# Products that nobody reads in TensorE's pauses around two routings, two layer norms and an RMS norm

## The chip, the cores and the metric

One Trainium2 chip, one core. The metric is the device time of one execution in microseconds (us). Three executions of the kernel before took 1819.88, 1822.99 and 1823.16 us; their median is 1822.99.

## What is computed

Two transformer blocks run one after the other on 256 tokens of 1024 values, all in float32. The first block mixes tokens with a gated delta rule and a spatial gating unit, and ends in a mixture of 32 experts. The second mixes them with two kinds of attention (16 heads), and ends in a mixture of 16 experts. What matters here is what stands ahead of each mixture:

```
x  = x + gate * merge_branches(...) @ w_o           # first block
hx = modulate(rms_norm(x, norm_ffn_g), shift, scale)
x  = x + gate * hier_moe(hx, ...)                   # 32 experts, 2 of them for each token
x  = rms_norm(x, final_norm_g)

h = token_mixer(x, ...)                             # second block
x = layer_norm_2(ALPHA * x + h, ln1_g, ln1_b)
h = grouped_moe(x, ...)                             # 16 experts, 2 of them for each token
x = layer_norm_2(ALPHA * x + h, ln2_g, ln2_b)
```

The two experts of a token are found from router logits (a product of the tokens with 36 or 16 columns), softmax and comparisons.

## The kernel before

Tokens lie along the free axis and the 1024 values in eight tiles (`KT = 8`) of 128 partitions. `X` holds the residual, `H` and `HS` the normed tokens and the squares. TensorE (`pe`), VectorE (`dve`), ScalarE (`act`), GpSimd (`pool`) and the DMA queue of SyncE (`sp`) each have a program of their own, written out by hand; semaphores (`s[...]`, `wait_ge`, `then_inc`) order them. TensorE executes its matmuls in the order of its program: whatever is put ahead of a wait is done before what stands behind it.

Every matmul goes through the helper `mm`, so that all of them have line L601 in the profile. A float32 product is two passes there: two LDWEIGHTS and two MATMULs.

Weights stream through a ring of nine slots of 1 MB (`ring`). `sp` loads the next slot when TensorE has released it (`slots_used`); with all nine full the queue stands still. The rows of experts that are chosen by rank are loaded only after VectorE has written the order (`order_ready`, L1818), in `count_tokens`.

The stretches that the change touches, in order of time:

- **First routing and gather**, `route(0, ...)` and the head of `mixture(0)`. After the last `norm_sum(0, 7)` ScalarE and VectorE make `H`, and a DMA brings `router_w`. TensorE then makes the logits (16 products with 36 columns, and two for the bias), 16 transposes of 128x128 (L958), waits for `kept` (L1887: the experts that each token keeps), makes five small products into bank 6 (`placed`), and waits while `place_tokens` and `make_gather` (L1828 to L1949) work out on VectorE which token goes where. `gather_x(0)` (16 products with 128 columns) collects the tokens of the first unit, VectorE and ScalarE copy them, and `up(0, 0)` and `up(0, 1)` begin the experts' work.
- **The first block's last norm**: eight `norm_sum(1, k)` (256 columns each, from L2043 by way of ScalarE's squares), then ScalarE and VectorE (L2048) norm `X`, and the second block's projections begin.
- **Attention's end**: four products with `sq_att` (512 columns), ScalarE's `heads_rnorm`, then the output projections, eight products each.
- **Second block's layer norm and routing**: `mean_sum(0, k)`, `variance_sum(0)`, then `route(1, ...)` and `mixture(1)`, built as the first. `X` comes from VectorE at L2137.
- **The last layer norm**: `mean_sum(1, k)`, `variance_sum(1)`, and the result is stored.

Bank 7 of PSUM is written by `gather_x` and `down`, and read only after these.

Of the kernel before, what the change touches and what calls it, by code (L numbers as in the profile page):

```python
# [211 lines left out]
def build(nc, t):  # L212

    ctx = ExitStack()
    with ctx:
        def sb(name, *shape):
            return ctx.enter_context(nc.sbuf_tensor(name, [P, *shape], F32))
# [10 lines left out]
        mats = sb("mats", len(MATS), P)  # L228
        ones = sb("ones", P)
# [8 lines left out]
        bank = [ctx.enter_context(nc.psum_tensor(f"bank{i}", [P, 512], F32)) for i in range(8)]  # L238
# [6 lines left out]
        def M(name):  # L245
            return mats[:, MATS.index(name), :]
# [352 lines left out]
        def _(pe):  # L599
            def mm(out, lhsT, rhs_, start=True, stop=True, **kw):  # L600
                return nc.tensor.matmul(out, lhsT, rhs_, start=start, stop=stop, **kw)  # L601
# [3 lines left out]
            def release(ins):  # L605


                nonlocal group_ended
                if group_ended:
                    ins.then_inc(slots_used, 1)  # L610
                group_ended = False
# [26 lines left out]
            def project_rows(acc, w, src, first):  # L638
# [6 lines left out]
                            release(ins)  # L645
                return ins

            def column_sum(out, src, n=KT):

                for k in range(n):  # L650
                    ins = mm(out, ones[:, :], src[:, k, :], k == 0, k == n - 1)
                    if k == 0:
                        release(ins)
                return ins

            pe.wait_ge(s["constants_set"], 4)

            pe.wait_ge(s["xc_squared"], 1)
            column_sum(bank[1][:, :], hc).then_inc(s["xc_summed"], 1)

            pe.wait_ge(s["cond_ready"], 1)
# [208 lines left out]
            n = 0  # L870
# [46 lines left out]
            def norm_sum(i, k):  # L917

                pe.wait_ge(s["norm_ready"], KT * i + k + 1)
                ins = mm(bank[4][:, 0:SEQ], ones[:, :], HS[:, k, :], k == 0, k == KT - 1)  # L920
                release(ins)
                if k == KT - 1:
                    ins.then_inc(s["norm_summed"], 1)
# [15 lines left out]
            def route(m, width, experts):  # L939


                pe.wait_ge(s["router_landed"], 16 * (m + 1))
                src = H if m == 0 else X
                logits = [bank[5][:, qt * width:(qt + 1) * width] for qt in range(QT)]
                for k in range(KT):
                    pe.wait_ge(s[f"route_in{m}"], k + 1)
                    for qt in range(QT):
                        mm(logits[qt], src[:, k, qt * P:(qt + 1) * P], router_w[m][:, k, :], k == 0 and qt == 0, False,
                           skip_group_check=True)
                at = D + (0, GROUPS1 + E1)[m]  # L950
                for qt in range(QT):
                    ins = mm(logits[qt], ones[0:1, :], one_row[0:1, 0, at:at + width], False, qt == QT - 1, skip_group_check=True)
                ins.then_inc(s["logits_made"], 1)

                for qt in range(QT):
                    for k in range(KT):
                        i = qt * 2 + k // 4
                        ins = nc.tensor.transpose(bank[i][:, (k % 4) * P:(k % 4 + 1) * P], src[:, k, qt * P:(qt + 1) * P],  # L958
                                                  M("ident"))
                        if k % 4 == 3:  # L960
                            ins.then_inc(s["rows_turned"], 1)

                pe.wait_ge(s["kept"], m + 1)
                pe.wait_ge(s["attn_landed"], 16)
                mm(bank[6][:, 0:experts], earlier, keep[:, 0, 0:experts])
                mm(bank[6][:, experts:2 * experts], earlier, keep[:, 1, 0:experts], True, False)
                mm(bank[6][:, experts:2 * experts], ones[:, :], keep[:, 0, 0:experts], False, True)
                mm(bank[6][:, 2 * experts:3 * experts], ones[:, :], keep[:, 0, 0:experts], True, False)
                mm(bank[6][:, 2 * experts:3 * experts], ones[:, :], keep[:, 1, 0:experts], False, True
                   ).then_inc(s["placed"], 1)  # L970

            def mixture(m):
# [9 lines left out]
                def gather_x(u):  # L982

                    pe.wait_ge(s["gather_made"], ub + u + 1)
                    for k in range(KT):
                        for qt in range(QT):
                            ins = mm(bank[6 + k // 4][:, (k % 4) * P:(k % 4 + 1) * P], own_rows[:, qt, k * P:(k + 1) * P],
                                     gather[u % 2][:, qt, :], qt == 0, qt == QT - 1)
                        if k % 4 == 3:
                            ins.then_inc(s["x_gathered"], 1)  # L990
# [59 lines left out]
                def combine_y(u):  # L1050
# [7 lines left out]
                                 combine[u % 2], u == 0 and j % 2 == 0, u == UNITS[m] - 1 and j % 2 == 1, skip_group_check=True)  # L1058
                    ins.then_inc(s["combined"], 1)

                pe.wait_ge(s["rows_copied"], 4 * (m + 1))
                gather_x(0)
                up(0, 0)
# [24 lines left out]
            def every_token(m):  # L1088
# [32 lines left out]
                ins.then_inc(s[f"all{m}_pe"], 1)  # L1121

            route(0, GROUPS1 + E1, E1)
            mixture(0)
            for k in range(KT):
                norm_sum(1, k)

            n2 = 0
            for j in range(O20):
# [100 lines left out]

            def variance_sum(i):

                for k in range(KT):
                    pe.wait_ge(s["ln_sq"], KT // 2 * i + k // 2 + 1)
                    ins = mm(bank[5][:, 0:SEQ], ones[:, :], HS[:, k, :], k == 0, k == KT - 1)
                ins.then_inc(s["ln_var"], 1)

            pe.wait_ge(s["heads_rnorm"], 8)
            for j in range(KT):
                if j >= 4:  # L1240
# [4 lines left out]
                if j > 0:  # L1245
                    mean_sum(0, j - 1)
            mean_sum(0, KT - 1)
            variance_sum(0)
            route(1, E2, E2)
            mixture(1)  # L1250
            for k in range(KT):
                mean_sum(1, k)
            variance_sum(1)


# [993 lines left out]
```

## Time and profile before

| | us |
|---|---|
| executions | 1819.88, 1822.99, 1823.16 |
| median | 1822.99 |
| the profiled execution, whole | 1820.98 |
| its span, first to last instruction | 1819.2 |
| TensorE busy | 1633.8 |
| VectorE busy | 553.0 |
| ScalarE busy | 322.6 |
| mean granted TensorE clock | 0.953 |

The page gives each engine's busy time and, in 40 slices of 45.5 us, TensorE's granted clock in tenths of full speed. The views used below are the timeline of TensorE (each line a group of like instructions, with the idle time ahead of it in brackets and what ended it), and the table of stretches, which gives for a stretch the busy time of each engine and the granted clock: 1.00 is 2.4 GHz and 0.50 is 1.2 GHz.

### The profile page before, as it was taken

What the parts mean: (1) busy time and instruction counts of PE and PEld (TensorE: products, weight loads), DVE (VectorE), ACT (ScalarE), POOL (GpSimd) and SP (SyncE); (2) the same over time, 40 slices, a digit from 0 to 9 for tenths busy, and PEclk for the clock granted to TensorE, in tenths of its full rate; (3) what the DMA queues carried; (4) which work ended last, traced back from release to release, by engine and by line L of the source; (5) the groups of instructions that cost most, each with busy time, mean ns of one, the idle gap of its engine ahead of it and who ended that gap; (6) DMA issues with size and microseconds to landing.
All of it is one profiled execution on the core that took longest, in us unless ns stands there. A gap on an engine that the chain in (4) does not pass through costs nothing.

```text
span 1819.2 us, 21572 instructions
## 1 busy us (share of the span) xinstructions
PE 1633.8 (90%) x8392; PEld 1057.2 (58%) x8392; DVE 553.0 (30%) x1120; ACT 322.6 (18%) x648; POOL 174.0 (10%) x180
## 2 busy tenths in 40 slices
PE   5799999999999989969998789988799998999985
PEld 1466666776588868855554369757534543443433
DVE  2266666666520011153122110382511111011002
ACT  2223333333231100011001021241100000000001
POOL 1144333334300000000000000000000000000000
PEclk8799999999999978969999899899699999999999
DMA  9311110111834413418999974103299989999993
GB/s 392 145 52 46 35 46 27 43 46 35 337 114 162 142 67 123 147 54 349 421 421 420 421 278 161 48 1 120 88 409 422 395 349 422 421 359 387 421 422 158
DMA packets 59644, 404.91 MB, mean 223 GB/s; under 512 B 6782, under 2 KB 7938, under 8 KB 13232
## 3 DMA queue, kind: packets, MB, share of 16 engines
q1 hardware_dynamic: 53328, 381.92, 52.7%
q0 software_dynamic: 6240, 21.92, 4.0%
q8 instruction: 55, 0.90, 0.2%
q14 instruction: 21, 0.17, 0.0%
HBM read 402.71 MB, written 1.10 MB: 222 GB/s over the span
## 4 chain that ended last, share of the span: by engine, by line
PE 70%; DMA 16%; DVE 9%; issue 2%; ACT 1%; SPq 0%; DVEq 0%; POOL 0%; POOLq 0%; ACTq 0%
PE bank L601 69%; DMA ring<-in_moe 14%; DVE arena L1619 2%; DMA ring<-in_dense 2%; ACT arena L1261 1%; DVE arena L1650 1%; DVE arena L1666 1%; PE bank L1017 1%; DVE arena L1655 0%; DVE arena L1647 0%; DVE arena L1645 0%; DVE arena L1659 0%; DMA arena<-in_router_w 0%; DMA arena<-decay_rows 0%; DVE arena L1669 0%
## 5 line engine op out<-in xcount | busy, mean ns | idle before, releaser
L601 PE MATMUL bank<-ring,arena 128*64 128x512 f32 (+2 forms) x2304 | 521.5, 606 | 58.6 <-DMA ring<-in_moe 56.9
L601 PE MATMUL bank<-arena 128*128 128x128 f32 (+3 forms) x2864 | 426.5, 300 | 35.2 <-DVE arena L1949 14.6
L601 PEld LDWEIGHTS bank<-arena 128*128 128x128 f32 (+2 forms) x2864 | 379.0, 194 | 134.0 <-ACT arena L1261 47.8
L601 PEld LDWEIGHTS bank<-ring,arena 128*64 128x64 f32 (+2 forms) x2304 | 174.6, 138 | 369.9 <-issue 364.9
L1261 ACT ACTIVATE arena<-bank 128x256 f32<-128x256 f32 (+1 forms) x369 | 164.1, 451 | 1186.0 <-PE bank L601 892.1
L601 PE MATMUL bank<-hc,head_w 128*128 128x512 f32 (+1 forms) x384 | 166.3, 541 | 3.0 <-DMA head_w<-in_head_w 3.0
L1971 DVE TENSOR_TENSOR arena<-arena,bank 128x256 f32<-128x256 f32 x48 | 20.2, 422 | 360.7 <-ACT arena L1261 360.7
L601 PE MATMUL bank<-arena,ring 128*128 128x256 f32 x512 | 116.6, 388 | 4.3 <-ACT arena L1261 2.6
L601 PEld LDWEIGHTS bank<-arena,ring 128*128 128x128 f32 x512 | 99.7, 195 | 19.7 <-ACT arena L1261 3.4
L601 PE MATMUL bank<-hc,ring 128*128 128x256 f32 x512 | 110.7, 380 | 0.0
L601 PEld LDWEIGHTS bank<-hc,ring 128*128 128x128 f32 x512 | 97.5, 190 | 12.9
L601 PEld LDWEIGHTS bank<-hc,head_w 128*128 128x128 f32 x384 | 66.2, 200 | 32.6 <-issue 30.3
L1261 ACT ACTIVATE arena<-arena 128x512 f32<-128x512 f32 (+3 forms) x152 | 73.9, 511 | 44.2 <-DVE arena L1871 13.1
L1967 DVE COPY arena<-bank 128x512 f32<-128x512 f32 x21 | 14.5, 692 | 210.9 <-PE bank L601 210.9
L550 POOL TENSOR_TENSOR arena<-arena,mats 128x512 f32<-128x512 f32 x48 | 68.3, 1430 | 103.3 <-PE bank L601 55.4
L1666 DVE TENSOR_TENSOR arena<-bank,mats 128x512 f32<-128x512 f32 x80 | 53.9, 689 | 49.5 <-PE bank L601 47.8
L1619 DVE SCALAR_TENSOR_TENSOR arena<-arena,vec 128x512 f32<-128x512 f32 (+1 forms) x72 | 62.6, 869 | 6.5 <-DVE arena L1617 1.2
L601 PE MATMUL bank<-xc,ring 128*128 128x256 f32 x256 | 55.7, 380 | 1.6 <-DVE xc L2048 1.6
L601 PEld LDWEIGHTS bank<-xc,ring 128*128 128x128 f32 x256 | 48.6, 190 | 8.4 <-issue 2.0
L601 PE MATMUL bank<-hc,ones 128*128 128x256 f32 (+1 forms) x80 | 27.6, 492 | 20.2 <-ACT hc L1261 20.2
L601 PE MATMUL bank<-arena,ones 128*128 128x512 f32 (+3 forms) x76 | 30.4, 521 | 9.9 <-ACT arena L1261 9.9
L1261 ACT ACTIVATE hc<-xc 128x256 f32<-128x256 f32 (+2 forms) x25 | 15.0, 613 | 128.7 <-DVE xc L1766 116.8
(241 smaller groups left out, 1056.7 us busy)
## 6 DMA issues: line engine op xcount, KB each, us to landing
ring<-in_moe SPq DMA_DIRECT2D x288, 1024.0 KB, 13.2
ring<-in_dense SPq DMA_DIRECT2D x72, 1024.0 KB, 7.0
head_w<-in_head_w POOLq DMA_DIRECT2D x27, 512.0 KB, 4.0
arena<-decay_rows POOLq DMA_DIRECT2D x16, 256.0 KB, 4.6
xc<-in_xc SPq DMA_DIRECT2D x1, 2048.0 KB, 8.6
arena<-bias_rows POOLq DMA_DIRECT2D x2, 1024.0 KB, 8.5
mats<-in_square SPq DMA_DIRECT2D x1, 1088.0 KB, 11.6
out_y<-xc SPq DMA_DIRECT2D x2, 512.0 KB, 2.9
```

Source lines behind the costliest of these rows:

```text
L550: nc.gpsimd.tensor_tensor(levels[k % 2], coupling, times(M(f"off{k}"), TT), ALU.mult).then_inc(s["level_masked"], 1)
L601: return nc.tensor.matmul(out, lhsT, rhs_, start=start, stop=stop, **kw)
L1017: ins = nc.tensor.transpose(bank[4 + step_no % 2][:, f * P:(f + 1) * P], hid[step_no % 2][:, f * P:(f + 1) * P], M("ident"))
L1261: return nc.scalar.activation(out, in_, func, **kw)
L1619: link(stt(c3, src, wgt, c3, ALU.mult, ALU.add))
L1650: stt(flat(conv[0]), flat(conv[0]), float(P) ** -0.5, flat(norms[0]), ALU.mult, ALU.mult).then_inc(s["normed"], 1)
L1666: tt_(group_of(picked, g), grown(g), times(M(f"pick{k + 1}"), 4), ALU.mult).then_inc(s["picked"], 1)
L1967: cp(x_cols[u % 2][:, 4:8, :].rearrange("p a b -> p (a b)"), bank[7][:, :]).then_inc(s["x_copied"], 1)
L1971: tt_(hid[step_no % 2], act_h[step_no % 2], bank[4 + step_no % 2][:, FS:2 * FS], ALU.mult).then_inc(s["hid_ready"], 1)
```

## The change

A helper `keep_warm(n)` does n products of `ones` (128x128) with 512 columns of the constant `mats`, into bank 7, with no wait and no semaphore; nobody reads the bank in between. It is called in eight places of TensorE's program, two of them in `route` and one in `mixture`, which each run twice, and one in `variance_sum`, which runs twice too: 22 products in all. No other engine's program changes.

```diff
+            def keep_warm(n):
+
+                for _ in range(n):
+                    mm(bank[7][:, :], ones[:, :], mats[:, 0:4, :].rearrange("p a b -> p (a b)"))
@@ route
+                keep_warm(2)
                 pe.wait_ge(s["router_landed"], 16 * (m + 1))
@@
+                keep_warm(1)
                 pe.wait_ge(s["kept"], m + 1)
@@ mixture
+                keep_warm(5)
                 pe.wait_ge(s["rows_copied"], 4 * (m + 1))
                 gather_x(0)
@@
             route(0, GROUPS1 + E1, E1)
             mixture(0)
+            keep_warm(1)
             for k in range(KT):
                 norm_sum(1, k)
+            keep_warm(1)
@@
             def variance_sum(i):
 
+                keep_warm(1)
                 for k in range(KT):
@@
+            keep_warm(2)
             pe.wait_ge(s["heads_rnorm"], 8)
             for j in range(KT):
```

## Rows read from the trace of the kernel before

**Rows 1.** The page: span, and TensorE's granted clock in 40 slices.
```profile
span 1819.2 us, 21572 instructions
...
PEclk8799999999999978969999899899699999999999
```

**Rows 2.** Stretches (start:end length, engines' busy us, clock, DMA share, GB/s).
```profile
790.00:820.00 30.00, 17.60 (x83) 14.37 (x84) 18.66 (x77) 4.29 (x8) 0.00 (x0) 0.65 0.00 1
...
827.00:1049.00 222.00, 199.46 (x1230) 106.99 (x1229) 48.44 (x111) 21.24 (x44) 0.00 (x0) 0.97 1.01 417
...
1275.00:1308.00 33.00, 24.22 (x112) 21.15 (x114) 18.94 (x79) 4.50 (x7) 0.00 (x0) 0.59 0.00 0
```

**Rows 3.** TensorE's timeline, first routing and gather (start, length, instruction, idle before).
```profile
778.35 0.70 PE L601 MATMUL bank<-hc,ones 128*128 128x256 f32 x2 [0.59 <-ACT hc L1261]
783.28 7.04 PE L601 MATMUL bank<-arena,hc 128*128 128x36 f32 x32 [4.24 <-DMA arena<-in_router_w]
...
791.25 3.40 PE L958 MATMUL bank<-mats,hc 128*128 128x128 f32 x16
797.55 1.00 PE L601 MATMUL bank<-arena,head_w 128*128 128x32 f32 x4 [2.90 <-DVE arena L1887]
...
808.54 6.75 PE L601 MATMUL bank<-arena 128*128 128x128 f32 x32 [8.71 <-DVE arena L1949]
```

**Rows 4.** Stretches of the first routing, with the clock.
```profile
780.00:781.00 1.00, 0.00 (x0) 0.00 (x0) 0.96 (x1) 0.01 (x1) 0.00 (x0) 0.79 0.92 385
...
783.28:791.25 7.97, 7.96 (x36) 7.83 (x37) 2.01 (x6) 0.00 (x0) 0.00 (x0) 0.50 0.14 59
...
794.00:795.00 1.00, 0.65 (x5) 0.41 (x3) 0.86 (x5) 0.00 (x0) 0.00 (x0) 0.88 0.00 0
...
799.85:808.54 8.69, 0.00 (x0) 0.03 (x1) 7.62 (x28) 0.14 (x1) 0.00 (x0) 0.50 0.00 0
```

**Rows 5.** Timeline at full clock: 128 columns; a weight load ahead of 512 columns.
```profile
823.10 3.84 PE L601 MATMUL bank<-arena 128*128 128x128 f32 x32
...
827.64 0.19 PEld L601 LDWEIGHTS bank<-arena,ones 128*128 128x128 f32 x1 [0.24 <-issue]
```

**Rows 6.** TensorE's timeline, the first block's last norm.
```profile
1062.65 5.41 PE L601 MATMUL bank<-hc,ones 128*128 128x256 f32 x16 [2.15 <-ACT hc L1261]
1069.68 27.87 PE L601 MATMUL bank<-xc,ring 128*128 128x256 f32 x128 [1.62 <-DVE xc L2048]
```

**Rows 7.** TensorE's timeline, attention's end and the output projection.
```profile
1227.46 3.70 PE L601 MATMUL bank<-arena,mats 128*128 128x512 f32 x8 [1.24 <-DVE arena L2117]
1233.74 8.86 PE L601 MATMUL bank<-arena,ring 128*128 128x256 f32 x32 [2.58 <-ACT arena L1261]
...
1242.87 3.62 PE L601 MATMUL bank<-arena,ring 128*128 128x256 f32 x16
```

**Rows 8.** TensorE's timeline, second layer norm, routing and gather.
```profile
1268.98 3.72 PE L601 MATMUL bank<-hc,ones 128*128 128x256 f32 x16 [1.86 <-ACT hc L1261]
1275.58 6.98 PE L601 MATMUL bank<-arena,xc 128*128 128x16 f32 x32 [2.88 <-DVE xc L2137]
...
1288.70 1.03 PE L601 MATMUL bank<-arena,head_w 128*128 128x16 f32 x4 [1.56 <-DVE arena L1930]
...
1296.86 6.65 PE L601 MATMUL bank<-arena 128*128 128x128 f32 x32 [5.85 <-DVE arena L1949]
```

**Rows 9.** Timeline of VectorE: the last tiles that the second router reads.
```profile
1277.58 1.38 DVE L2137 TENSOR_SCALAR xc<-xc,vec 128x256 f32<-128x256 f32 x4
```

**Rows 10.** Stretches within a run of products with 32 columns, early in the kernel.
```profile
52.00:56.00 4.00, 4.00 (x38) 4.00 (x37) 0.00 (x0) 0.00 (x0) 0.00 (x0) 1.00 1.00 418
57.00:59.00 2.00, 2.00 (x11) 2.00 (x11) 0.00 (x0) 0.00 (x0) 0.00 (x0) 0.50 0.42 172
```

**Rows 11.** TensorE's timeline, the last layer norm.
```profile
1800.31 3.72 PE L601 MATMUL bank<-xc,ones 128*128 128x256 f32 x16 [1.75 <-DVE xc L2144]
1805.90 3.72 PE L601 MATMUL bank<-hc,ones 128*128 128x256 f32 x16 [1.86 <-ACT hc L1261]
```

## The prediction

> **What bounds the kernel now.** I read the page first: the granted clock is near full in most slices, and lowest (7, 8, 6 of ten) early and where the two routings lie [rows 1]. The table of stretches shows what a routing is: VectorE and TensorE take turns, and the DMA engines move nothing for 30 us in the first and 33 us in the second, since the ring is full [rows 2]. Behind the first routing they run without a pause (share 1.01) for 222 us [rows 2]. So the mixtures are bound largely by transfers, and these restart only when TensorE frees slots and VectorE, behind the gather's copy, gives the experts' order. A microsecond saved before the first slot is freed moves the stream by as much. I count it in full.
>
> The timeline and the clock then show what a microsecond could come from. After 778.35 + 0.70 TensorE has nothing for 4.24 us [rows 3]; the clock falls within that pause (0.79 in its second microsecond), and the router runs at 0.50 [rows 4]. The transposes lift it (0.88 in the microsecond in which they end), the pause for `kept` loses it again, and the gather after 8.71 us of pause starts at half [rows 3, 4]. Its 32 passes take 6.75 us, where 32 of the same shape take 3.84 at full clock [rows 3, 5]. The second routing repeats this [rows 8].
>
> **The price of a product.** Two passes of 512 columns, each spaced by 0.24 + 0.19 = 0.43 us at full clock [rows 5]: 0.86 us; at half clock, by the ratio 6.75 to 3.84 and its limit of two, 1.5 to 1.7 us; I take 1.7. Five are 4.3 us at full and 8.6 at half. They are only free as long as they end before what TensorE waits for. They have no wait, so TensorE can be late but nobody else is held directly; what they write is read by nobody.
>
> **Part by part.** Where a part is given with two bounds, the first is what it can save at most (the clock stays full), the second what it costs if the clock does not move.
>
> - *Two products ahead of the first router.* Pause 4.24 us [rows 3], they fill 1.7 (3.4 at half): hidden. They put off the fall of the clock, which came about 1.6 us into the pause. Most: the 36 passes take 7.97 us at half [rows 4], so 4.0; cost 0. But early in the kernel the clock fell in the midst of 64 passes much like the router's (38 in 4 us, then 11 in 2 us) while TensorE was never idle [rows 10], so it may fall within the router too. I take 1.3.
> - *One ahead of `kept`, twice.* Pauses of 2.90 and 1.56 us [rows 3, 8]. Saves nothing by itself: what follows are five products whose result VectorE takes later. At half it fills 1.7 us, so in the second routing it can be 0.15 late. Bounds 0 and -0.15; I take 0.
> - *Five ahead of the first gather.* Pause 8.71 us; they take 4.3 to 8.6: hidden in every case, by 0.1 us at least. Most: the gather takes 3.7 instead of 6.75 [rows 3, 5], so 3.1. If they start at half clock, as here [rows 4], I expect them to lift it as the transposes did (0.88 in the microsecond in which these end [rows 4]), and they end some 2 us before the gather, which then starts at full. If they start at full they end 4.4 us before it, longer than the pause in which the clock fell ahead of the router. I take 2.0.
> - *One before and one behind the sums of the norm.* Pauses of 2.15 and 1.62 us [rows 6] against 0.86, or 1.7 at half. The 16 passes took 5.41 us, where 16 of that shape take 3.72 after a pause of 1.86 [rows 6, 8]; the clock fell in the first and not in the second. Most 1.7, cost 0.1. I take 1.7: one product leaves 1.3 us of pause.
> - *Two at attention's end.* Pause 2.58 us [rows 7]; two products take 1.7 there (3.4 at half, 0.8 late). The first 32 passes of the output projection took 8.86 us, the next 16 3.62 [rows 7], so 32 take 7.2. Most 1.7, cost 0.8; I take 1.7.
> - *One in the variance sums and two ahead of the second router.* Pauses 1.86 and 2.88 us [rows 8] against 0.86 and 1.7 at full: hidden; at half 3.4 against 2.88, 0.5 late. The sums already ran at full, 3.72. The router's 36 passes took 7.9 us; but the last tiles it reads come at 1277.58 + 1.38 = 1278.96 [rows 9], and eight passes and the bias follow, so at most 3.0. For the same reason as in the first I take 1.3.
> - *Five ahead of the second gather.* The pause is 5.85 us [rows 8]. At full they end 1.5 us early; at half all through they would be 2.7 late; lifted half way, they need between (4.3 + 8.6)/2 = 6.5 and less, 0.6 late. Most: the gather 3.0 shorter; cost 2.7. I take 2.5 less 0.6 = 1.9. Its small products for `placed` end at 1291.01 and VectorE waited some tenths for them; at full they give 0.1.
> - *The last layer norm.* Both sums ran at full, 3.72 us after pauses of 1.75 and 1.86 [rows 11]: 0, and 0 late even at half.
>
> Sum against the profiled execution: 1.3 + 2.0 + 1.7 + 1.7 + 1.3 + 1.9 + 0.1 = 10.0 us. All bounds of savings together are 16.6, all costs 0.1 + 0.15 + 0.8 + 0.5 + 2.7 = 4.3.
>
> **From the profiled execution to the median.** That execution took 1820.98 and its span 1819.2. In it the clock fell at both of the short pauses where it need not: a pause of 2.15 us lost it ahead of the norm's sums, one of 2.58 at attention's end, while 1.75, 1.86 and 1.86 kept it [rows 6, 7, 8, 11]. In other executions the fall can come at other places, so I count these two at half for the median: 10.0 - 1.7 = 8.3. That gives 1822.99 - 8.3 = 1814.7 from the median and 1820.98 - 8.3 = 1812.7 from the profiled one; I take **1814.5**, nearer the median since that is what is measured.
>
> The Trainium skill bears on this last step. Its page "TensorE: Matmul & The Clock Gate", section "Part 1: The HAM clock gate", says that the moments at which the clock may change are not tied to the start of the kernel, so that one kernel shows another number of slow products in each run. By that rule no sum made from one execution holds in full, and the 10.0 would be 8 or less. One trace can't show it; like pauses with unlike ends (2.15 and 1.86 us) agree with it.
>
> **The rivals.**
>
> *The clock is lost again.* The products end early and the rest of the pause still loses it, ahead of both routers and of one gather, or it falls within the router, as it did in [rows 10]. For: the five run at full end 4.4 us ahead of the first gather. Against: they start at half in the trace, and so end late. What is left are the two norm parts at half, 1.7, one gather 2.0 and 1.2 elsewhere: 4.9, so 1818.1.
>
> *The transfers take the gain back.* The first experts' work starts earlier but the stream, at 417 GB/s for 222 us [rows 2], sets the end and starts no earlier. Then only the norms' parts (1.7 at half) and tenths remain: 1821. Against: the engines stand idle for 30 us before, with the ring full, and what restarts them is behind the gather.
>
> *Slower.* The added products run at half and do not lift the clock. Then each stretch keeps its slow matmuls and gets the overruns: 2.7 us ahead of the second gather first of all, then 0.8 and 0.5, in sum 4.3: 1827.3. It decides from the point at which the five need more than 5.85 us and the gather behind them is not faster, that is, when under 2.7 us of it comes back. Against: it rose while TensorE did transposes, from 791.25 to the microsecond at 794 [rows 3, 4].
>
> **How the numbers follow.** Under 0.2% (3.6 us) can't be told from no change. Forecast (6 to 12 us less, 1811 to 1817): 0.62. Clock lost again (1816.5 to 1821): 0.22, of which 0.13 is faster by over 0.2%. Transfers: 0.11, nearly all within 0.2%. Slower: 0.05. Faster 0.76, same 0.19, slower 0.05. The range goes from 1808.5 (the forecast with two more of the 6.6 us up to the bound of the savings, and the favourable executions) to 1820.0, which takes in most of the first rival and leaves out the other two.
>
> **What would show it.** In the profile after: the gathers at 3.7 us in place of 6.75 and 6.65; the norm's 16 passes at 3.7 for 5.41; the output projection's first 32 at 7.2; the clock's slices at the routings up; the router still partly at half; the idle ahead of the second gather gone, with VectorE's L1949 done some tenths before it. The prediction is wrong if the clock does not rise during the five products, if the gathers start at half, or if the stream of transfers restarts as late as before relative to `norm_sum(0, 7)`.

## The result

Five executions of the changed kernel took 1801.98 to 1807.39 us, median 1805.57; five of the kernel before 1816.44 to 1823.16, median 1819.88. The ratio is 0.9922, 95% interval 0.9902 to 0.9943: some 14.3 us less. I had forecast 1814.5 within 1808.5 to 1820.0: a saving of 8.3 us, from a start of 1822.99. The direction was right and the size too small: the measured time lies below the range.

The profiled execution of the changed kernel has a span of 1800.2 us, 19.0 less than the profiled one before. The page (span, granted clock in 40 slices):

```profile
span 1800.2 us, 21660 instructions
...
PEclk8799999999999988989999999999999999999999
```

The slices of the clock in which the two routings lie, 6 and 6 before [rows 1], are 8 and 9. (The 7 and the 8 ahead of the first 6 belong to the spatial gating unit, 637 to 728 us.) The timeline of TensorE (start, length, instruction, idle before) answers to [rows 3]; the products added are the lines that read `mats` and `ones`:

```profile
779.04 1.88 PE L601 MATMUL bank<-mats,ones 128*128 128x512 f32 x4
783.41 5.81 PE L601 MATMUL bank<-arena,hc 128*128 128x36 f32 x32 [2.49 <-DMA arena<-in_router_w]
...
793.62 1.73 PE L601 MATMUL bank<-mats,ones 128*128 128x512 f32 x2
796.45 0.63 PE L601 MATMUL bank<-arena,head_w 128*128 128x32 f32 x4 [1.10 <-DVE arena L1899]
...
797.59 6.24 PE L601 MATMUL bank<-mats,ones 128*128 128x512 f32 x10
807.44 5.44 PE L601 MATMUL bank<-arena 128*128 128x128 f32 x32 [3.62 <-DVE arena L1961]
813.66 7.09 PE L601 MATMUL bank<-ring,arena 128*64 128x512 f32 x32 [0.79 <-DVE arena L1979]
```

The router starts when it did (783.28 before) and takes 1.2 us less, and the gather takes 5.44 us for 6.75: not the 3.7 of full clock. The five products ended 3.6 us ahead of it. The table of stretches (start:end length, busy us of five engines, granted clock, DMA share, GB/s) shows that the clock is full at the pause's end and falls within the gather:

```profile
806.00:807.00 1.00, 0.00 (x0) 0.00 (x0) 0.89 (x4) 0.00 (x0) 0.00 (x0) 1.00 0.00 0
807.50:811.00 3.50, 3.50 (x22) 3.50 (x23) 0.00 (x0) 0.89 (x2) 0.00 (x0) 0.67 0.02 5
```

The norm and attention's end, for [rows 6, 7], and the second routing, for [rows 8]:

```profile
1057.82 3.72 PE L601 MATMUL bank<-hc,ones 128*128 128x256 f32 x16 [1.29 <-ACT hc L1273]
...
1221.71 7.17 PE L601 MATMUL bank<-arena,ring 128*128 128x256 f32 x32 [0.86 <-ACT arena L1273]
...
1261.88 1.93 PE L601 MATMUL bank<-arena,xc 128*128 128x16 f32 x16 [1.17 <-DVE xc L2149]
1264.34 2.04 PE L601 MATMUL bank<-arena,xc 128*128 128x16 f32 x16 [0.53 <-DVE xc L2149]
...
1280.56 3.81 PE L601 MATMUL bank<-arena 128*128 128x128 f32 x32 [2.20 <-DVE arena L1961]
1285.15 5.37 PE L601 MATMUL bank<-ring,arena 128*64 128x512 f32 x24 [0.78 <-DVE arena L1979]
```

The sums take 3.72 for 5.41, the projection's first 32 passes 7.17 for 8.86, the gather 3.81 for 6.65. The second router now waits for VectorE in its middle (0.53): it ran ahead of it.

Where the 19.0 us between the two spans lie, by how far like instructions are apart: router 1.2, first gather 1.3, norm 1.7, attention's end 1.7, second router 2.5, `placed` and second gather 3.0: 11.4 in the stretches with products. Another 7.9 are elsewhere: 2.4 in the first mixture and 5.5 in attention, 4.5 of these at its entry and 1.0 near its end; 0.3 were lost again here and there. At the entry the first kernel had half clock for 13.7 us and the changed one none:

```profile
1163.00:1176.00 13.00, 12.22 (x28) 7.42 (x28) 6.81 (x14) 4.63 (x9) 0.00 (x0) 0.50 0.00 1
```

```profile
1155.00:1169.00 14.00, 11.24 (x45) 7.20 (x46) 11.89 (x23) 5.88 (x11) 0.00 (x0) 1.00 0.01 1
```

(the first of the kernel before, the second of the changed one). The nearest product that was added ahead of this place ends some 90 us before it.

### The profile page after: what moved, and what is told of

Read it like the earlier page. It is cut to its first block, busy times and chain, and to the rows that moved or that the text cites. A ratio compares the mean times of both kernels' runs of the same rounds, so it can differ in the third digit from the quotient of the medians.

```text
span 1800.2 us, 21660 instructions
## 1 busy us (share of the span) xinstructions
PE 1632.9 (91%) x8436; PEld 1048.4 (58%) x8436; DVE 552.9 (31%) x1120; ACT 323.0 (18%) x648; POOL 173.7 (10%) x180
## 4 chain that ended last, share of the span: by engine, by line
PE 69%; DMA 17%; DVE 9%; issue 3%; ACT 1%; SPq 0%; DVEq 0%; POOL 0%; POOLq 0%; ACTq 0%
PE bank L601 68%; DMA ring<-in_moe 14%; DVE arena L1631 2%; DMA ring<-in_dense 2%; ACT arena L1273 1%; DVE arena L1662 1%; DVE arena L1678 1%; PE bank L1024 1%; DVE arena L1667 0%; DVE arena L1659 0%; DVE arena L1657 0%; DVE arena L1671 0%; DMA arena<-in_router_w 0%; DVE xc L2147 0%; DMA arena<-decay_rows 0%
## 5 line engine op out<-in xcount | busy, mean ns | idle before, releaser
L601 PEld LDWEIGHTS bank<-arena 128*128 128x128 f32 (+2 forms) x2864 | 374.1, 192 | 125.8 <-ACT arena L1273 47.8
L601 PE MATMUL bank<-arena 128*128 128x128 f32 (+3 forms) x2864 | 421.0, 297 | 26.4 <-DVE arena L1681 6.8
```

## The experiments

Each kernel was timed against the kernel before on the same chip. The two theories at the start: **each product acts where it stands**, and its part can be measured alone; or **part of the difference is chance or acts from afar**.

**The kernel before again.** No edit.

> The kernel before, unchanged, profiled a second time. Of the 19.0 us between the two profiled spans some 6 lie where no product was added: 4.0 us at the entry of attention (half clock from 1162.87 for 13.7 us before, full clock after) and 2.3 us at the end of the first mixture (half clock at 1039.99). Theory 1 (chance): those falls come and go between executions of one kernel. Then this profile shows the short falls at other places than the first one; the ones in the two routings stay. Theory 2 (lasting): the kernel before always loses the clock at attention's entry, and the products remove that from afar; then the fall at the entry stands here again. The ratio is 1.000 within 0.2% by both.

Measured: ratio 1.0012 (0.9996 to 1.0028). Half clock stands at attention's entry again:

```profile
1160.20:1173.80 13.60, 12.82 (x30) 7.93 (x30) 7.26 (x14) 4.63 (x9) 0.00 (x0) 0.50 0.00 1
```

This spoke for the second theory. The 29 executions of the kernel before in this comparison have a median of 1817.99, and those of the later ones 1817.4, 1820.0 and 1819.0. The 1822.99 from which I started is the median of three at the upper end.

**The gathers' products alone.** From the changed kernel, all calls but `keep_warm(5)` taken out.

```diff
-                keep_warm(2)          # route
-                keep_warm(1)          # route
                 keep_warm(5)
-            keep_warm(1)              # both of the norm
-                keep_warm(1)          # variance_sum
-            keep_warm(2)              # attention's end
```

> Only the five products ahead of each mixture's first gather (10 of 22). Theory 1 (each product acts where it stands): from the two profiles the gathers gave 1.3 and 2.9 us, so 4 us less than before, ratio 0.9977; the first gather at about 3.8 us for 6.75, the second near 3.8 for 6.65; the routers still at half. Theory 2 (the products act as a whole, or from afar): nearly the full 14 us, ratio 0.992, or nearly none.

Measured: 0.9979 (0.9965 to 0.9993), 3.8 us less, as the first theory has it. Alone, the five bring the first gather to full clock, since they start later and at half, and end 2 us ahead of it:

```profile
806.50 3.81 PE L601 MATMUL bank<-arena 128*128 128x128 f32 x32 [2.04 <-DVE arena L1961]
...
1289.10 3.73 PE L601 MATMUL bank<-arena 128*128 128x128 f32 x32
```

**Without the gathers' products.**

```diff
-                keep_warm(5)
```

> The changed kernel without the five products ahead of each gather (12 of 22 remain). Theory 1 (each acts where it stands): the change's 14.3 us less 4, so about 10 us less than before, ratio 0.9943; both gathers again at 6.7 us. If the whole is worth more than its parts, this and the run with the gathers' products alone give less than 14 us in sum.

Measured: 0.9944 (0.9922 to 0.9967), 10.2 us less. With the 3.8 above it makes the 14 of the whole. I had expected both gathers at 6.7 us. The first takes 5.53 us here, hardly more than the 5.44 with the five: in these profiles the five buy almost nothing at the first gather; at the second they do (6.17 here, 3.81 with them):

```profile
807.64 5.53 PE L601 MATMUL bank<-arena 128*128 128x128 f32 x32 [9.47 <-DVE arena L1961]
...
1284.15 6.17 PE L601 MATMUL bank<-arena 128*128 128x128 f32 x32 [6.75 <-DVE arena L1961]
```

**Narrow products.** All 22 in their places, with 16 columns.

```diff
-                    mm(bank[7][:, :], ones[:, :], mats[:, 0:4, :].rearrange("p a b -> p (a b)"))
+                    mm(bank[7][:, 0:16], ones[:, :], mats[:, 0, 0:16])
```

> All 22 products in their places, each with 16 columns in place of 512: same count of instructions, next to no work for the array. Theory 1 (the work keeps the clock): no gain, ratio 1.000, half clock in both routings. Rival (the gain comes from the instructions ahead of the waits, as that weights are loaded or the queue is filled): 14 us less as with the wide ones.

Measured: 0.9986 (0.9971 to 1.0002), no gain that can be told from none. The router after its narrow products takes its 7.04 us as before, the second gather 6.39. It is the work of the products that holds the clock, not that instructions stand there. Two things did change: the first gather took 5.18 us for 6.75, and attention's entry ran at full, with nothing changed near it. By its span this profile is 6.1 us under that of the kernel before, 4.5 of them at the entry, while the executions together give 2.5 us (none to 5.3). So one profile can overstate a gain.

```profile
783.71 7.04 PE L601 MATMUL bank<-arena,hc 128*128 128x36 f32 x32 [3.87 <-DMA arena<-in_router_w]
...
1291.12 6.39 PE L601 MATMUL bank<-arena 128*128 128x128 f32 x32 [3.72 <-DVE arena L1961]
```

```profile
1160.00:1174.00 14.00, 11.59 (x47) 7.23 (x47) 11.92 (x22) 5.88 (x11) 0.00 (x0) 1.00 0.00 1
```

**The changed kernel again.** No edit.

> The changed kernel, unchanged, measured and profiled again. Its gain on record, 0.9922, rests on five runs of each; the kernel before has now 29 with a median of 1818.0, under the 1819.9 of those five. If the parts add up as they stand (gathers 3.8, all the rest 10.2) the ratio is again 0.9922 to 0.9925. Under the rival that the first five runs happened on favourable positions it is 0.9945 or more. In the profile: both gathers at 3.8 us; a fall at attention's entry may stand or not, no product is near it.

Measured: 0.9925 (0.9911 to 0.9939). The gain on record stands: 13.6 us of 1817.4. The second gather took 3.81 us, but the first 5.44 again, where I had expected 3.8. It is not always so. Two later kernels, the two with eight products ahead of the spatial gating unit, have the same products at the first routing, and its gather took 6.38 us in one profile and 3.81 in the other; with the norm's products alone, and so none anywhere ahead of the gather, it took 5.18 (in this order):

```profile
805.09 6.38 PE L601 MATMUL bank<-arena 128*128 128x128 f32 x32 [5.31 <-DVE arena L1962]
```

```profile
816.22 3.81 PE L601 MATMUL bank<-arena 128*128 128x128 f32 x32 [1.96 <-DVE arena L1963]
```

```profile
806.50 5.18 PE L601 MATMUL bank<-arena 128*128 128x128 f32 x32 [8.80 <-DVE arena L1961]
```

Two things follow. With the five in place, the pause that is left behind them goes with the result: 1.96 and 2.04 us left, 3.81 for the gather; 3.62, 5.44; 5.31, 6.38. And without them the first gather is no fixed point: 6.6 to 6.8 us in five profiles (the kernel before three times, attention's end alone, norm and attention's end), 5.2 in three (norm alone, narrow, variance and `kept` alone). So the 1.3 us between the two profiles at this place can't be credited to the five. The second gather is clear: 3.7 to 3.8 us in all eight profiles with the five or the ten, 5.3 and more in all ten without them or with narrow ones.

**The routers' products alone.**

```diff
                 keep_warm(2)
-                keep_warm(1)          # and the five other calls
```

> Only the two products ahead of each router (4 of 22). From the two profiles the routers gave 1.1 and 2.5 us. Theory 1 (each acts where it stands): 3.5 us less than before, ratio 0.998; router 1 ends about a microsecond earlier after its start at 783.3, router 2 two and a half; the gathers still at 6.7. Rival (the clock falls within the router anyway): under 1 us.

Measured: 0.9985 (0.9976 to 0.9993), 2.7 us less. The rival, under 1 us, is out. The two routers take 6.37 us and 1.93 + 3.14.

**Norm and attention's end alone.**

```diff
-                keep_warm(2)          # route; and those of kept, gather and variance_sum
             keep_warm(1)              # both of the norm
             keep_warm(2)              # attention's end
```

> Only the products around the sums of the first block's last norm (one before, one behind) and the two at attention's end (4 of 22). From the two profiles they gave 1.7 and 1.6 us. Theory 1: 3.3 us less, ratio 0.9982, the sums at 3.7 us for 5.4 and the projection's first passes at full. Rival (in most executions the clock does not fall at these short pauses, as I took for the median): half of that, 1.7 us, 0.9991.

Measured: 0.997 (0.9954 to 0.9986), 5.4 us less, more than the 3.3 to be seen at the two places, though the interval takes 3.3 in. The halving that I used for the median, 1.7 us, lies outside it (2.5 to 8.4). In the profile 1.7 us were lost again behind attention's end: the second block's variance sums took 5.41 us for 3.72. Attention's entry, on the other hand, ran at full there, so more than the two places is in the 5.4.

**The rest alone: one ahead of `kept`, one ahead of the variance sums.**

```diff
-                keep_warm(2)          # route
                 keep_warm(1)          # route
-                keep_warm(5)
-            keep_warm(1)              # both of the norm
                 keep_warm(1)          # variance_sum
-            keep_warm(2)              # attention's end
```

> The rest of the change: only the product ahead of each kept wait and the one ahead of each variance sum (4 of 22). The parts measured so far are 3.8 (gathers), 2.7 (routers) and 5.4 us (norm and attention's end), 11.9 of 13.6. Theory 1 (these four do nothing by themselves, as forecast; the missing 1.7 is uncertainty or comes from the parts acting together): ratio 1.000 to 0.9995. Rival (they carry the missing 1.7 us): 0.999.

Measured: 0.9987 (0.9971 to 1.0002). It decides nothing: 2.4 us less, or none.

**Ten in place of five.**

```diff
-                keep_warm(5)
+                keep_warm(10)
```

> The changed kernel with ten products in place of five ahead of each gather. Ten take 8.6 us at full clock and more where they start at half; the pauses are 8.7 and 5.85 us. Theory (overruns cost one for one): the first gather at most 2 us later, the second 3 to 5 us later, in sum 4 to 6 us more than the changed kernel, ratio 0.9955 to 0.9965. Rival (the stream of transfers has room and takes the delay in, as would be if the transfers bound the mixtures from elsewhere): no change, 0.9925.

Measured: 0.9922 (0.99 to 0.9945), the same as with five, and my theory of 4 to 6 us more fell. Nor was it the rival's room in the transfers. The profile shows a gain and a loss:

```profile
796.11 10.53 PE L601 MATMUL bank<-mats,ones 128*128 128x512 f32 x20
806.47 3.73 PE L601 MATMUL bank<-arena 128*128 128x128 f32 x32
...
1274.91 8.83 PE L601 MATMUL bank<-mats,ones 128*128 128x512 f32 x20
1283.57 3.73 PE L601 MATMUL bank<-arena 128*128 128x128 f32 x32
```

In the first pause they end 0.5 us later than the gather began with five (counted from their own start, the gather begins after 10.4 us for 9.9), and the gather takes 3.73 for 5.44, 1.7 us less. In the second they end 1.9 us later (8.7 for 6.7), where I had expected 3 to 5: they ran at full there. By these rows the sum is 0.7 us more, too little to be told from the same. I had not seen that the first gather still had something to give.

**The norm's products alone, and attention's end alone.**

```diff
             keep_warm(1)              # both of the norm; all others out
```

```diff
             keep_warm(2)              # attention's end; all others out
```

> Only the two products around the sums of the first block's last norm. In all five profiles without them the clock fell within the 16 sums, in none of the five with them. Theory (the fall comes each time, so it counts in full): 1.7 us less, ratio 0.9991. Rival (most of the 5.4 us of norm and attention's end lies here, the second product holding the clock into the projections): 0.998 or less.

> Only the two products at attention's end. The clock fell in the first passes of the output projection in all five profiles without them, in none with them. Theory (it counts in full): 1.7 us less, ratio 0.9991. Rival (most of the 5.4 us lies here): 0.998 or less.

Measured: attention's end 0.9991 (0.9971 to 1.001), as expected but with a wide interval; the norm 0.9965 (0.9949 to 0.998), that is 6.4 us (3.6 to 9.3), the rival's size. The norm's profile shows the 1.7 us at the sums, and nothing of what the rival says of the projections behind, which ran at full without the product too. What differs is attention's entry, at full here, as it also is with the narrow products and with those of variance and `kept` alone:

```profile
1058.30 3.72 PE L601 MATMUL bank<-hc,ones 128*128 128x256 f32 x16 [1.30 <-ACT hc L1273]
...
1221.79 8.86 PE L601 MATMUL bank<-arena,ring 128*128 128x256 f32 x32 [2.58 <-ACT arena L1273]
```

```profile
1150.00:1166.00 16.00, 12.78 (x50) 7.66 (x49) 10.61 (x20) 7.82 (x15) 0.00 (x0) 1.00 0.00 1
```

With attention's end alone the two lines change places: sums slow, projection fast, and half clock at the entry:

```profile
1061.95 5.41 PE L601 MATMUL bank<-hc,ones 128*128 128x256 f32 x16 [2.14 <-ACT hc L1273]
...
1233.02 7.17 PE L601 MATMUL bank<-arena,ring 128*128 128x256 f32 x32 [0.86 <-ACT arena L1273]
```

```profile
1162.10:1175.80 13.70, 12.92 (x31) 7.92 (x30) 7.48 (x15) 4.72 (x10) 0.00 (x0) 0.50 0.01 1
```

What attention's end gains here does not last. The second block's variance sums, at full in the kernel before (3.72 us [rows 8]), lose the clock behind it and give the 1.7 us back:

```profile
1266.58 5.41 PE L601 MATMUL bank<-hc,ones 128*128 128x256 f32 x16 [1.86 <-ACT hc L1273]
```

It was the same with norm and attention's end together. In the eight profiles that have wide products at attention's end and one ahead of these sums, they took 3.72. So the one ahead of the variance sums, which I had counted as nothing, is what lets attention's end keep its gain; that rests on two profiles against eight, and no run took out this product alone.

**The kernel before a third time.** No edit.

> The kernel before, profiled a third time. If the falls ahead of the norm's sums and in the output projection come in every execution, both stand here too (3.4 us of half clock each); if they come in part of them, as I took for the median, there is an even chance for each. At attention's entry half clock for 13.7, 3.4 or no us shows that this place is the one that varies.

Measured: 1.0002 (0.9983 to 1.002). Both short falls stand here, and half clock at the entry once more:

```profile
1162.40:1175.90 13.50, 12.72 (x30) 7.73 (x29) 7.36 (x14) 4.83 (x10) 0.00 (x0) 0.50 0.00 1
```

Three experiments went on from there to places that the change left out.

**Eight more ahead of the spatial gating unit.** It waits 8.94 us for `v_normed` and its products run at half.

```diff
+            keep_warm(8)
             pe.wait_ge(s["v_normed"], 1)
```

> The changed kernel with eight more products in the longest pause that is left without any, 8.94 us ahead of the spatial gating unit's 32 products (wait for v_normed), whose 64 passes run at half clock, 0.36 us each, 23.4 us in all. The eight take 6.9 us at full and are hidden. Theory A (the clock, once kept, stays through these products): they take about 12 us, 11 us less than the changed kernel, ratio near 0.9865. Theory B (half of these products have one row only and the clock falls within them): up to 2 us less, 0.991 to 0.9925.

Measured: 0.993 (0.9915 to 0.9944), nothing beyond the changed kernel: the first passes ran at full, 0.21 us each, and then the clock fell while TensorE was busy without a break.

```profile
662.75:663.70 0.95, 0.95 (x5) 0.71 (x6) 0.00 (x0) 0.00 (x0) 0.00 (x0) 1.00 0.00 0
663.80:684.40 20.60, 20.60 (x58) 14.16 (x57) 2.97 (x7) 0.00 (x0) 0.00 (x0) 0.50 0.00 1
```

**And one of 384 columns behind each of the unit's eight steps.**

```diff
                 ins.then_inc(s["sgu_mixed"], 1)
+                mm(bank[7][:, 0:384], ones[:, :], mats[:, 0:3, :].rearrange("p a b -> p (a b)"))
```

> The changed kernel with eight products ahead of the spatial gating unit, as in the run before, and one of 384 columns (0.64 us at full clock) behind each of its eight steps. With the eight alone the clock fell about a microsecond into the unit, and its 64 passes kept 0.36 us each; the first four took 0.21. Theory (some wide work in between keeps the clock): 64 x 0.21 = 13.4 us and 8 x 0.64 = 5.1 us in place of 23.1: 4.6 us less than the changed kernel, ratio near 0.990. Rival (the clock falls all the same): the added products run at half, 8 x 1.3 = 10 us more, ratio 0.998.

Measured: 0.9879 (0.9854 to 0.9903). Median 1798.9, but the profiled execution took 1813.3, and in it the clock fell all the same. The four others took 1795.5 to 1799.8 at a mean granted clock of 0.974 to 0.978, against 0.966 in the profiled one. By that, both the theory and the rival came true, in different executions of one kernel.

**Two more at attention's entry.**

```diff
                 pe.wait_ge(s["sb_logs"], a + 1)      # ahead of it:
+                if a == 0:
+                    mm(bank[5][:, :], ones[:, :], mats[:, 0:4, :].rearrange("p a b -> p (a b)"))
                 pe.wait_ge(s["dl_probs"], a + 1)     # ahead of it:
+                if a == 0:
+                    mm(bank[5][:, 0:256], ones[:, :], mats[:, 0:2, :].rearrange("p a b -> p (a b)"))
```

> The changed kernel with two more products at attention's entry, into bank 5, which is free there: 512 columns in the pause of 1.42 us ahead of the first head's sb_logs, 256 columns ahead of its dl_probs. Half clock at the entry lasted 13.7 us in both profiles of the kernel before, 3.4 in four others and none in four, with no product near it. Theory 1 (it comes and goes, and a product there holds the clock): no half clock at the entry, ratio 0.9915 to 0.9925, since the changed kernel seldom loses much there. Rival (the added work is late and costs): 0.9930 or more.

Measured: 0.9906 (0.9885 to 0.9927), not to be told from the changed kernel's 0.9925. Half clock at the entry for 3.4 us stood in the profile nevertheless, so the theory's first half is wrong: one product there does not rule it out. The fall came at 1158.3, between the first (1151.7) and the second (1159.4).

**All of it, with ten ahead of the unit.** The edits of the last two, and `keep_warm(10)` ahead of `v_normed`.

> The changed kernel, ten products (8.6 us at full) in place of eight in the pause of 8.94 us ahead of the spatial gating unit, one of 384 columns behind each of its eight steps, and the two at attention's entry. With eight, a pause of 2.07 us was left ahead of the unit; in the profiled execution (1813.3 us) the clock fell all the same, while the four others took 1795 to 1799. Theory (the pause that was left decides it): the unit at full in the profile, 13.4 + 5.1 us, every execution under 1800, ratio 0.986 to 0.988. Rival (it is the unit's own products): still half clock in some executions, times in two groups, 1798 and 1813.

Measured: 0.9869 (0.9845 to 0.9893), five executions from 1794.4 to 1798.6, the fastest kernel of the study, 0.6% under the changed one by the two ratios. The pause ahead of the unit is 0.36 us, and the unit runs at full:

```profile
664.60:683.00 18.40, 18.40 (x80) 12.38 (x81) 3.40 (x8) 0.00 (x0) 0.00 (x0) 1.00 0.00 1
```

against, in the kernel with eight and the pause of 2.07 us,

```profile
665.50:690.00 24.50, 24.50 (x60) 15.71 (x60) 2.55 (x6) 0.00 (x0) 0.00 (x0) 0.50 0.00 1
```

Five executions in one group, after five in two, speak for the pause as what decides; they don't prove it.

## Why the prediction was right and wrong

**The mechanism** was right: products of 512 columns in the pauses hold the clock, products of 16 do not, and the microseconds go through to the end. Of the rivals, *slower* never showed; *transfers take it back* is out, since from the first experts' products to the last norm the changed kernel gained 2.4 us more instead of losing what it had; *the clock is lost again* was right at the first gather, and in other kernels at the variance sums.

**Where the 8.9 us lie** by which 1805.6 is under 1814.5: 2.9 in the start, 1.7 in the halving of two terms, 1.4 in the sizes at the places with products (11.4 between the profiles for 10.0 taken), and 2.9 elsewhere, where I had put nothing.

**The start.** The median of three was 1822.99, that of the five beside the changed kernel 1819.88. I treated the median of three as a fixed point when its own spread was 3.3 us, and chose the forecast nearer to it than to the profiled execution. Moved down by these 3.1 us, the lower end of the range would have been 1805.4, just at the measured time. The two profiles, 19.0 us apart, overstate the change: that of the changed kernel is the fastest of its five executions, 3.6 us under their median, and that of the kernel before is 1.1 above its own.

**The terms**, against the two profiles and against what each part gave alone:

| term | taken | between the profiles | alone, 95% |
|---|---|---|---|
| first router | 1.3 | 1.2 | with the second: 2.7 (1.3 to 4.4) |
| second router | 1.3 | 2.5 | |
| first gather | 2.0 | 1.3 | with the second: 3.8 (1.3 to 6.4) |
| second gather, `placed` | 2.0 | 3.0 | |
| norm's sums | 1.7, then 0.85 | 1.7 | 6.4 (3.6 to 9.3) |
| attention's end | 1.7, then 0.85 | 1.7 | 1.6 (none to 5.3) |
| `kept`, variance sums | 0 | 0 | 2.4 (none to 5.3) |
| elsewhere | 0 | 7.9 | |

*The step from the profiled execution to the median failed.* I halved the norm's and attention's end, since pauses of like length had kept the clock. In all eight profiles without a wide product at the norm (the kernel before three times; attention's end alone; narrow; gathers alone; routers alone; variance and `kept` alone) the clock fell within its sums, and in none of the ten with one. At attention's end it fell in all eight without wide products and in none of the ten with them. A pause of 2.15 us here was no coin toss. That 1.86 us kept the clock was: at the variance sums such a pause kept it in six profiles and lost it in three (5.41, 5.41 and, with narrow products, 5.30 us). The Trainium skill's page "TensorE: Matmul & The Clock Gate", section "Part 1: The HAM clock gate", says that where the clock changes against the kernel's start differs from run to run. The profiles agree in part: the fall ahead of the router came at 780.6, 777.9 and 780.0 in three of the same kernel. But the work had moved with it: the last `norm_sum` began at 778.35, 775.88 and 777.88, so that the fall came 2.0 to 2.3 us behind that each time, and the router took its 7.04 us in all three. And I drew from the page that a fall may stay away, which it does not say and the rows deny at these places.

*Second router and second gather were undersized*, by 1.2 and 1.0 us. The router held full clock up to its end, and I had charged 0.6 us for an overrun: by the time the five started, `placed` ended at full (0.82 us for its last six, 1.44 before), so they ran at full, 4.54 us, and fitted into the pause.

*The first gather was oversized*, by 0.7, for the same reason turned round: the five started near full and ended 3.6 us too soon. I had named this as a risk and not seen that the routers' products make it likely. Ten there brought the gather to 3.73 us. Even the 1.3 is not surely theirs, since the gather took 5.2 us in three profiles without them.

*Elsewhere* I had put nothing, and gave no reason for it, though [rows 1] shows an 8 in two slices without products: 1001 to 1046 us, the end of the first mixture, and 1137 to 1183 us, attention's entry. Half clock at the entry lasted 13.7 us in four of the eighteen profiles, 3.4 in six and none in eight. The four are those in which TensorE does nothing up to this place that it did not do before: the kernel before three times, and attention's end alone. In the fourteen with any product added ahead, even of 16 columns or only the one ahead of the first `kept`, it was never 13.7, and the entry took 3.3 to 4.6 us less than in the first profile. So it does not take the norm's products to remove this fall. A shift of the work against the moments at which the clock changes could do it, and so could chance; no run shifted the work alone, and the cause stays open. Nor need every execution of the kernel before have this fall: 13.7 us at half are 0.004 of the mean granted clock, and its executions lie between 0.951 and 0.960, but those at the upper end were not profiled. In the profile with the norm's products alone the sums and the entry together give 1.7 + 4.6 = 6.3 of the 6.4 us; since the narrow products' profile has 4.5 at the entry too and its executions only 2.5 (none to 5.3), that sum may be luck.

*Two readings of the rows were off.* The slices of 7 and 8 ahead of the first routing are the spatial gating unit, whose 23 us at half clock I had passed over. And the second routing does not repeat the first in all: there the transposes did not lift the clock, which stayed at half from 1275.5 to 1302.8:

```profile
1283.46:1287.14 3.68, 3.67 (x17) 3.27 (x16) 2.77 (x15) 2.02 (x4) 0.00 (x0) 0.50 0.00 0
```

So "as the transposes did" was no ground for the five at the second gather. That they lift it from half is shown by the gathers' products alone (3.81 and 3.73 us).

## What to carry to other kernels

Before costing a change to the clock, take the profile of the unchanged kernel two or three times: the falls that come each time are worth their full price, those that move about are not, and one profile can't tell them apart; nor is a median of three a fixed point when single executions are 3 us apart. Size the filling by what pause is left ahead of the work that matters, at the clock that the filling will really have, not by how much fits at half clock. And ask whether the work that follows loses the clock again, as the spatial gating unit did while TensorE was busy, and the variance sums did behind attention's end.

## What the runs showed that I had not expected

- The clock fell while TensorE was busy throughout: in the spatial gating unit, half of whose products have a single row, a microsecond after its start. Its 64 passes take 0.21 us each at full clock and 0.36 at half, 13.4 against 23.1 us. With a product of 384 columns behind each step it was held in the profile that had a pause of 0.36 us ahead, and lost in the one with 2.07 us; by their times and mean clocks the other four executions of each kernel held it.
- Nearly all executions of the kernel before lay between 1810 and 1825 us, a spread as wide as the whole gain of the change (13.6). Half clock at attention's entry, 13.7 us in some profiles and none in others, made 4.5 us of difference between the first two profiles.
